# Hybrid decoder trunk on one core: weights streamed in three half chunks, and a ring of eleven slots

## What is computed

```
for layer in range(2):
    hn = rmsnorm(h, attn_norm[layer])
    mix = pool_attention_mixer(...) if layer % 2 == 0 else ssd_mixer(...)
    h = h + mix
    h = h + peer_ffn(rmsnorm(h, ffn_norm[layer]), ...)
```

```
u = expert_u[idx]
act = gelu(einsum('nhkd,nd->nhk', u, xb))
coef = gate * act
out = einsum('nhk,nhkd->nd', coef, expert_v[idx])
```

## Time and profile before

| | |
|---|---|
| median of 3 runs | 1641.92 us (1640.35 to 1643.54) |
| profiled execution | 1642.93 us, span in the profile 1641.1 us |
| TensorE matmul | 1191.8 us busy, 73% |
| VectorE | 1174.9 us, 72% |
| GpSimd | 590.9 us, 36% |
| ScalarE | 522.6 us, 32% |
| DMA | 665.99 MB, mean 406 GB/s |
| of it gathers and other GpSimd DMAs | 540.65 MB, 79.8% of the DMA time |
| of it SP's queue, mostly weights | 123.46 MB, 17.9% |
| granted TensorE clock, mean | 0.869 of full speed |

### The profile page before, as it was taken

One profiled execution on the slowest core, in us unless ns is written; L12 is line 12 of the kernel. 1 busy time (PEld: TensorE's weight loads), 2 busy tenths in 40 slices (PEclk: granted clock), 3 DMA queues, 4 the chain that ended last, 5 costly groups with the idle time before them and its releaser, 6 DMA issues.

```text
span 1641.1 us, 21546 instructions
## 1 busy us (share of the span) xinstructions
PE 1191.8 (73%) x7384; PEld 579.4 (35%) x7384; DVE 1174.9 (72%) x3348; ACT 522.6 (32%) x1207; POOL 590.9 (36%) x525
## 2 busy tenths in 40 slices
PE   8876685768748885978785798599597955555555
PEld 3552232225405662432263366344134611111111
DVE  3557868776678778897665877689966577777755
ACT  0132134222223563642132256355211322222211
POOL 1043333534433223323333432232343444444451
PEclk9987898989968997998998799799798977787776
DMA  9599999999999999999999999999999999999996
GB/s 378 245 375 422 423 423 421 421 422 422 422 412 382 422 423 409 397 422 424 420 423 422 400 422 423 423 403 402 366 412 423 421 421 421 421 421 421 421 421 263
DMA packets 84076, 665.99 MB, mean 406 GB/s; under 512 B 9376, under 2 KB 9520, under 8 KB 10752
## 3 DMA queue, kind: packets, MB, share of 16 engines
q0 software_dynamic: 74608, 540.65, 79.8%
q1 hardware_dynamic: 9216, 123.46, 17.9%
q10 hardware_dynamic: 144, 0.52, 0.1%
HBM read 663.55 MB, written 1.05 MB: 405 GB/s over the span
## 4 chain that ended last, share of the span: by engine, by line
DMA 30%; PE 28%; DVE 26%; ACT 7%; issue 7%; POOL 2%; DVEq 0%; POOLq 0%; ACTq 0%; SPq 0%
DMA ring<-in_experts,idx 30%; PE acc L846 11%; DVE ring L1453 9%; PE act_bank L551 6%; PE dve_bank L537 6%; DVE scratch L1097 3%; ACT L884 2%; DVE onehot L1097 2%; POOL ring L480 2%; ACT scratch L884 2%; ACT diag L1031 1%; DVE scratch L1269 1%; PE act_bank L537 1%; ACT scratch L958 1%; PE act_bank L773 1%
## 5 line engine op out<-in xcount | busy, mean ns | idle before, releaser
L480 POOL DMA_INDIRECT ring<-in_experts,idx x512 | 584.9, 1142 | 1005.3 <-PE acc L846 789.8
L846 PE MATMUL acc<-ring,diag 64*64 64x512 f32 x4096 | 617.8, 731 | 362.3 <-ACT diag L1031 340.6
L1453 DVE CUSTOM_DVE_ANT_0 ring<-ring,hn 128x1024 f32<-128x1024 f32 x512 | 622.4, 1224 | 267.3 <-DMA ring<-in_experts,idx 247.8
L846 PEld LDWEIGHTS acc<-ring,diag 64*64 64x64 f32 x4096 | 155.6, 154 | 723.3 <-ACT diag L1031 468.1
L1024 ACT ACTIVATE acts<-dots 128x2 f32<-128x2 f32 x256 | 52.0, 203 | 720.9 <-DVE dots L1453 703.0
L551 PE MATMUL act_bank<-hnT,wbuf 128*128 128x128 f32 x1856 | 235.3, 285 | 24.9 <-ACT scratch L958 17.4
L551 PEld LDWEIGHTS act_bank<-hnT,wbuf 128*128 128x128 f32 x1856 | 221.8, 198 | 76.3 <-issue 76.3
L1031 ACT ACTIVATE diag<-cst,coefs 128x64 f32<-128x64 f32 x512 | 150.2, 340 | 226.1 <-DVE coefs L1461 191.7
L884 ACT ACT_TABLE_LOAD x80 | 102.6, 1283 | 19.2 <-DMA rowc<-in_rows 16.9
L1461 DVE TENSOR_TENSOR coefs<-acts,gate 128x2 f32<-128x2 f32 x256 | 41.3, 161 | 74.4 <-ACT acts L1024 54.7
L1024 ACT ACT_TABLE_LOAD x68 | 87.2, 1283 | 5.9 <-ACT scratch L884 0.4
(11 more groups left out here) (143 smaller groups left out, 911.2 us busy)
## 6 DMA issues: line engine op xcount, KB each, us to landing
wbuf<-in_weights SPq DMA_DIRECT2D x50, 2048.0 KB
ring<-in_weights SPq DMA_DIRECT2D x5, 2048.0 KB, 19.8
ring<-in_experts,idx POOLq DMA_INDIRECT x512
kept<-in_weights SPq DMA_DIRECT2D x2, 2048.0 KB, 23.6
wbuf<-in_weights SPq DMA_DIRECT2D x2, 1024.0 KB, 7.5
scratch<-in_bias POOLq DMA_DIRECT2D x1, 1024.0 KB, 11.5
scratch<-in_bands POOLq DMA_DIRECT2D x1, 768.0 KB, 13.4
h<-in_x SPq DMA_DIRECT2D x1, 512.0 KB, 4.2
```

The source lines that it names most:

```text
L480: pool.indirect_dma_start(ring[:, n % RING], None, io[f"experts{layer}"], bass.IndirectOffsetOnAxis(idx[:, at:at + 1], 0),).then_inc(sem(f ...
L846: last[rows] = pe.matmul(acc[rows][half][home:home + HALF_P], diag[part, n % DIAGS], ring[part, slot, D + half * CW:D + (half + 1) * CW], ...
L1453: dve.tensor_tensor_reduce(out=ring[:, slot, 0:D], in0=ring[:, slot, 0:D], in1=hn[:, phase % NBLK], scale=1.0, scalar=0.0, op0=ALU.mult, o ...
```

## The change

The two whole buffers become three half buffers of 1 MB (8 KB in each partition). A chunk is loaded by two DMAs, and the halves go round the three buffers. TensorE raises `halves_free` by one for each half that it has read: for the first half on the matmul that reads its last part, for the second where `chunks_free` was raised before. Half m may be loaded once m - 2 releases have come, which is when half m - 3 is read. Chunks read by rows are halved by k. Chunks read by columns (queries and convolution) are stored in memory so that each half holds 256 columns. The 1 MB set free is the eleventh slot of the ring. The first chunk goes to the halves, and chunks 1 to 5 to the ring (chunk 1 was in `wbuf` before, and chunk 6, the first query chunk, in the ring). In the query stage TensorE now also waits for its own product after an even head, before the release.

```diff
-RING = 10
+RING = 11
 GROUP = 2
...
-NWB = 2
+HALVES = 3
 L0_CHUNKS = 4 + 2 + 4
...
-    streamed = 0
+    halves = 0
     for layer in range(DEPTH):
...
                     yield "kept", layer
-                    continue
-                n = streamed
-                streamed += 1
-                if n < NWB:
-                    yield "wbuf", n
-                elif n < NWB + STAGED:
-                    yield "ring", n - NWB
+                elif layer == b == 0 and 1 <= c <= STAGED:
+                    yield "ring", c - 1
                 else:
-                    yield "wbuf", n - STAGED
+                    yield "halves", halves
+                    halves += 2
...
         gains = sb("gains", D)
-        wbuf = sb("wbuf", NWB * CH).rearrange("p (n k c) -> p n k c", n=NWB, k=KD)
+        half_buf = sb("half_buf", HALVES * CH // 2).rearrange("p (n c) -> p n c", n=HALVES)
         ring = sb("ring", RING * 2 * D).rearrange("p (r d) -> p r d", r=RING)
-        staged = ring.rearrange("p (n r) d -> p n (r d)", r=2)
-        kept = sb("kept", CH).rearrange("p (k c) -> p k c", k=KD)
+        staged = ring[:, 0:2 * STAGED].rearrange("p (n r) d -> p n (r d)", r=2)
+        kept = sb("kept", CH)
         cst = sb("cst", C_END)
...
                             sp.wait_ge(sem("bias_loaded"), 16)
-                        if t == 0:
-                            flat = wbuf[:, 0].rearrange("p k c -> p (k c)")
-                            sp.dma_start(flat[:, 0:CH // 2], w[:, 0:CH // 2]).then_inc(sem("half_chunk_in"), 16)
-                            sp.dma_start(flat[:, CH // 2:], w[:, CH // 2:]).then_inc(sem("chunk_in0"), 16)
-                        elif kind == "ring":
+                        if kind == "ring":
                             sp.dma_start(staged[:, n], w).then_inc(sem(f"staged_in{n}"), 16)
...
                                     sp.wait_ge(sem("kept_used"), layer * NBLK)
-                                sp.dma_start(kept.rearrange("p k c -> p (k c)"), w).then_inc(sem("kept_in"), 16)
+                                sp.dma_start(kept, w).then_inc(sem("kept_in"), 16)
                         else:
-                            if n >= NWB:
-                                sp.wait_ge(sem("chunks_free"), n - NWB + 1)
-                            sp.dma_start(wbuf[:, n % NWB].rearrange("p k c -> p (k c)"), w
-                                         ).then_inc(sem(f"chunk_in{n % NWB}"), 16)
+                            for part in range(2):
+                                m = n + part
+                                if m >= HALVES:
+                                    sp.wait_ge(sem("halves_free"), m - HALVES + 1)
+                                sp.dma_start(half_buf[:, m % HALVES], w[:, part * CH // 2:(part + 1) * CH // 2]
+                                             ).then_inc(sem(f"half_in{m % HALVES}"), 16)
                         t += 1
...
         def _(pool):
-            pool.wait_ge(sem("half_chunk_in"), 16)
+            pool.wait_ge(sem("half_in0"), 16)
             pool.dma_start(rowc, io["rows"].to_broadcast([P, 2 * HD + 3 * SH])).then_inc(sem("rows_loaded"), 16)
-            pool.wait_ge(sem("chunk_in1"), 16)
+            pool.wait_ge(sem("staged_in0"), 16)
             pool.dma_start(bias_t, io["bias"].rearrange("p (h k) -> p h k", h=HEADS)).then_inc(sem("bias_loaded"), 16)
...
-                if n % GROUP == 0:
+                if n >= RING and (n - RING) % GROUP == 0 or n == RING:
                     for rows in range(2):
-                        pool.wait_ge(sem(f"pairs_summed{rows}"), n // GROUP + 1)
+                        pool.wait_ge(sem(f"pairs_summed{rows}"), (n - RING) // GROUP + 1 + AHEAD)
                 if n % TOPK == 0:
                     pool.wait_ge(sem("idx_ready"), n // TOPK + 1)
-                if n < RING and n % 2 == 0:
+                if n < 2 * STAGED and n % 2 == 0:
                     pool.wait_ge(sem("staged_free"), n // 2 + 1)
...
-            def next_chunk():
+            class Chunk:
+                def __init__(self, kind, n, by_rows):
+                    self.kind, self.n, self.by_rows, self.seen = kind, n, by_rows, -1
+                    if kind == "kept":
+                        pe.wait_ge(sem("kept_in"), 16 * (n + 1))
+                    if kind == "ring":
+                        pe.wait_ge(sem(f"staged_in{n}"), 16)
+                def half(self, part):
+                    m = self.n + part
+                    if self.kind == "halves":
+                        if part > self.seen:
+                            self.seen = part
+                            pe.wait_ge(sem(f"half_in{m % HALVES}"), 16 * (m // HALVES + 1))
+                        return half_buf[:, m % HALVES]
+                    flat = kept if self.kind == "kept" else staged[:, self.n]
+                    return flat[:, part * CH // 2:(part + 1) * CH // 2]
+                def __getitem__(self, key):
+                    k = key[1]
+                    if self.by_rows:
+                        return self.half(k // (KD // 2)).rearrange("p (k c) -> p k c", k=KD // 2)[:, k % (KD // 2)]
+                    part, first = divmod(key[2].start, CW // 2)
+                    return self.half(part).rearrange("p (k c) -> p k c", k=KD)[:, k, first:first + P]
+                def first_half_read(self, ins):
+                    if self.kind == "halves":
+                        ins.then_inc(sem("halves_free"), 1)
+            def next_chunk(by_rows=True):
                 kind, n = HOMES[chunks[0]]
                 chunks[0] += 1
-                if chunks[0] == 1:
-                    pe.wait_ge(sem("half_chunk_in"), 16)
-                    return wbuf[:, 0]
-                if kind == "kept":
-                    pe.wait_ge(sem("kept_in"), 16 * (n + 1))
-                    return kept
-                if kind == "ring":
-                    pe.wait_ge(sem(f"staged_in{n}"), 16)
-                    return staged[:, n].rearrange("p (k c) -> p k c", k=KD)
-                pe.wait_ge(sem(f"chunk_in{n % NWB}"), 16 * (n // NWB + 1))
-                return wbuf[:, n % NWB]
+                return Chunk(kind, n, by_rows)
...
                 kind = HOMES[chunks[0] - 1][0]
-                pe.sem_inc(sem({"ring": "staged_free", "wbuf": "chunks_free", "kept": "kept_used"}[kind]), 1)
+                pe.sem_inc(sem({"ring": "staged_free", "halves": "halves_free", "kept": "kept_used"}[kind]), 1)
...
                                     stop=last and k == tiles[-1])
+                    if k == KD // 2 - 1 and w is not dtw:
+                        w.first_half_read(ins)
                     if tick is not None and k % 2 and k < tiles[-1]:
...
                                         start=k == 0, stop=k == KD - 1)
+                    if j == 1 and len(tiles) > 2:
+                        w.first_half_read(ins)
                 return ins
...
-                def other_half():
-                    if b == 0:
-                        pe.wait_ge(sem("chunk_in0"), 16)
...
                     ins = yield from row_products(out, hnT, w, tick=T_IN0 + 4 * c,
-                                                  halfway={0: other_half, 3: first_scores}.get(c))
+                                                  halfway=first_scores if c == 3 else None)
                     ins.then_inc(sem(kind + "_full"), 1)
...
                                    bcT[:, (d - 4) * 4:(d - 3) * 4].rearrange("p g t -> p (g t)"), 4)
-                    w = next_chunk()
+                    w = next_chunk(by_rows=False)
                     out = fill("act")
...
                                 ins = pe.matmul(out_z, hnT[:, k], w[:, k], start=k == 0, stop=k == KD - 1)
+                                if k == KD // 2 - 1:
+                                    w.first_half_read(ins)
                     if g < SG and g % 2:
...
                     if hd % 2 == 0:
-                        w = next_chunk()
+                        w = next_chunk(by_rows=False)
                     out = fill("act")
...
                     ins.then_inc(sem("act_full"), 1)
-                    if hd % 2:
+                    if hd % 2 or w.kind == "halves":
                         chunk_used("act")
...
+def by_column_halves(chunks):
+    n = len(chunks)
+    return chunks.reshape(n, P, KD, 2, CW // 2).transpose(0, 1, 3, 2, 4).reshape(n, P, CH)
...
         consts[:, C_GAIN + layer * KD:C_GAIN + (layer + 1) * KD] = tiles_last(a["attn_norm"][layer])
-    weights = [chunked(np.concatenate([q_and_k, pooled, v], axis=1)), chunked(a["even_w_out"][0]), chunked(a["peer_w_q"][0]),
-               chunked(w_in[:, SI:SI + XBC]), chunked(w_in[:, 0:SI]), chunked(a["ssm_w_out"][0]),
-               chunked(a["peer_w_q"][1])]
+    weights = [chunked(np.concatenate([q_and_k, pooled, v], axis=1)), chunked(a["even_w_out"][0]), by_column_halves(chunked(a["peer_w_q"][0])),
```

(2 more changed lines are left out.)

## The result

The changed kernel takes 1645.8 us (median of 20 executions, 1643.3 to 1648.1), the kernel before on the same chips 1643.3 us (20 executions): ratio 1.0018, 95% interval 1.0011 to 1.0024. It is some 3 us slower, where I had forecast 7.1 us faster. The profiled execution took 1648.1 us, with a span of 1646.3 us.

What follows compares the result with a forecast made beforehand. The prediction took the DMA engines, at 422 GB/s, to bound the kernel. Slot -9.6, weights' room +2.5 and other terms 0 summed to -7.1 us, so a median of 1634.8 us, range 1626 to 1644.

Steps and rivals of the forecast that it cites:

- the first dip: DMA rate below 422 GB/s from 480 to 510 us: 5.0 us lost, forecast to shrink to about 2.5 us.
- The slot: Eleventh ring slot: one more gather allowed ahead, worth at most 2.48 us once per stretch, together 9.6 us saved.
- A: Stretch from 474.6 to 548.9 us where no dot product waits for a gather: 5.0 us lost, 2.48 us to win.
- B: Stretch from 626.4 to 763.4 us where no dot product waits for a gather: 3.9 us lost, 2.48 us to win.
- D: Stretch from 1053.0 to 1193.7 us where no dot product waits for a gather: 10.6 us lost, 2.48 us to win.
- C: Stretch from 899.0 to 971.9 us where no dot product waits for a gather: 2.1 us lost, all to win.
- The room of the weights: Three half chunks of room for four: one half load moves from the idle start into full DMA time, plus 2.48 us.
- the old gap: DMA idle time at the start, from 64 us to the first gather at 84.19 us; weights were forecast to move there.
- Halving and the number of transfers: Weight loads: a half chunk costs 2.48 us at 422 GB/s like a gather, and 50 more DMAs cost nothing.
- rival 3: Halves come late in the 16 convolution chunks, TensorE waits 0.5 us for each of 32: +16 us, 1651 us; chance 0.13.
- Rival 1: In the stretches, half a chunk less ahead takes back 0 to 5 us of the slot's 9.6: 1639.4 to 1644.4; chance 0.20.
- Rival 2: In the dips, more comes back: half of the remaining 12 us gives 1628.8, all of it 1622.8 us; chance 0.15.

Runs made afterwards that it cites:

- the second run: The changed kernel run once more, unchanged, beside the kernel before, with a second profile taken: ratio 1.0023 (1.0014 to 1.0033).
- after: The changed kernel (three half buffers, eleven slots) against the kernel before: 1645.8 us, ratio 1.0018.
- the pair with the lighter convolution: Changed kernel with two of three convolution taps on VectorE left out, against the kernel before: 1.0026 with ten slots, 0.9999 with eleven.
- four halves: Changed kernel with four half buffers and ten slots, the memory of the kernel before, only halved: 1647.5 us, ratio to before 1.0029.
- two halves: Changed kernel with two half buffers and twelve slots: ratio to the kernel before 1.0107 (1.0091 to 1.0122).

## Why the prediction was wrong, point by point

**What bounds the kernel.** That the DMA is the level at which it runs, and that only idle DMA time can be won, held. What failed is the yardstick: "each as length times (1 - rate / 422)". This is the mean over 16 engines, and a gather waits for the last of them. By the last parts, of the 5.0 us that I gave to the first dip, 2.3 were time of the last engine; of the 2.1 of the third, 0.7. The rest was time of the engines ahead, and filling it brought nothing here. The deeper ring made it plain: the first dip filled up to 404 GB/s, gathers took 19.4 us from issue to landing for 16.8 with ten slots, and the time hardly moved.

**The slot, -9.6 forecast, -4.1 measured** (-3.3 by the second run). The failed step is "A, B and D: 2.48 us each; C: 2.1 us". A and C gave nothing. B and D gave about 5 us by the landings, of which D alone 3.5 (3.9 with the second profile of after, 4.2 in the pair with the lighter convolution): more than one gather, against my "once, however many dips the stretch has". The stretches are not of fixed length either. With ten slots and three halves D ran from 1057.1 to 1198.1 us, with eleven from 1056.2 to 1205.5. A stretch ends where the engines have used up what had landed ahead, so another slot makes it longer. Halving moves it too: B took 137.0 us before, 142.6 with ten slots and three halves.

**The room of the weights, +2.5 forecast, +2.3 measured.** Right within a wide interval, and the mechanism is in the traces. The 101 GB/s in the old gap, which I had named as its sign, don't show it: four halves move them too, and they have the old room. What shows it is the bytes: when the first gather lands, SP's queue has moved 21.7 MB before and with four halves, and 20.7 MB with three, one half chunk less. SP issued the missing half at 92.2 us (forecast 91.5). From there on, with 2.49 us for each half chunk set off, three halves run 1.6 us behind four at the first gather, 2.2 at gather 145 and 1.8 at the last (the least between them is -0.2, at gather 280).

**Halving and the number of transfers, 0 forecast, +4.8 measured.** The failed step is that a half "costs the same 2.48 us" beside the gathers: I took 422 GB/s for any mixture of pieces, though the row for it (100 to 480 us) is mostly gathers. In the stretches of the weights before had 423, and every kernel with 8 KB pieces whose loads were in time 420 or 421. Over the two stretches shown that is 1.6 us, and 6.1 us of packet time over the whole run; that it is the whole of the 4.8 us is argued, not shown. Nor is the number of transfers settled: a second DMA for each chunk adds 1.8 us by the ratios, which the intervals can't tell from nothing. The fixed cost that the Trainium skill ("DMA: Bandwidth & Descriptors", Anatomy of one DMA) gives, about 2.0 us for each DMA on GpSimd's path, would make an estimated 100 us of 50 more if it were exposed. These loads are on SyncE's, and two DMAs for each chunk cost 3.3 us in all. With this term and the slot as measured the sum is +3.0; with the slot as forecast it would have been -2.3.

**Halves in time, 0 forecast.** Right. No wait for `half_buf` appears on TensorE, and rival 3 is refuted for three halves; two halves show it. Where a half loads, the weights had 56.9% of the DMA time in 533 to 536 us and 52.4% in 539 to 542, near the half that I had expected. Queues, changed kernel, 539 to 542 us:

```profile
q1 hardware_dynamic: 80, 0.66, 52.4%
q0 software_dynamic: 81, 0.61, 49.2%
```

The Trainium skill's rule ("DMA: Bandwidth & Descriptors", Queues, rings and completion order) that an engine goes round its queues packet by packet agrees with it. In the kernel before I read 72.2% against 28.4% as such turns, near two to one. It is 2.5 to one, 94 packets of 16 KB against at most 71 of 8 KB, so in those 5 us the turns were not one for one.

**TensorE's additions, 0 forecast.** Not isolated. TensorE's idle time ahead of the key products, which follow the new wait, went from 35.4 to 41.1 us (before, then after):

```profile
L827 PE MATMUL act_bank<-keysT,scratch 128*128 128x128 f32 x128 | 23.0, 304 | 35.4 <-issue 25.5
L844 PE MATMUL act_bank<-keysT,scratch 128*128 128x128 f32 x128 | 24.4, 318 | 41.1 <-ACT scratch L901 28.2
```

That is inside my bound of 8.1 us. Whether any of it reached the time no run tells; it would be part of the 4.8 us. The 0.1 us that I gave each new wait stands in no row.

**The rivals.** Rival 1 gave 1639.4 to 1644.4 by a trade of room against slot. The trade is there (2.3 against 4.1 us), but it isn't what made the kernel slower. Rival 2 is refuted: B and D kept their dips.

## What to carry to other kernels

A transfer spread over 16 DMA engines is done when the last part is in: read a dip in the mean GB/s only after the landings of first and last parts, since it may be engines ahead that wait for the one behind, and then more depth fills the dip and not the time. Before cutting a stream into smaller pieces, read the rate in a stretch where it is mixed with the other traffic, not the rate of that traffic alone. And when room is moved from one buffer to another, take apart the cutting, the room lost and the room won in runs of their own: here they were +4.8, +2.3 and -4.1 us, none of which the total of +3 would have told.

## What the runs showed of the hardware

- Pieces of 16 KB beside gathers of 8 KB: 423 GB/s. Pieces of 8 KB: 420 to 421. Pieces of 4 KB: 392 to 394, though there loads were late too (DMA share 0.98 for 1.01).
- The parts of a gather land mostly 2 to 9 us apart (at most 12.2), and while the queues never run empty the gap doesn't close: in the last phase it went from 3.7 to 8.5 us in the changed kernel. 48 packets of 0.61 us, by all signs on one engine, opened it to 12.7 us, and the run took 28.3 us longer.
- Queue q8 brings TensorE's instructions, one packet of 16 KB for 280 increments. Some q8 packets coincide with a slip of some 1 us in the part of one engine. Queue q14 brings instructions of SyncE, 21 packets of 8 KB for some 5200 waits, which cost nothing that could be measured (1.0002). The steps of 1 us in the gap of the last phase come with packets of q14 beside which a gather packet takes 0.97 us for 0.31; no run isolates their price.
- Sixteen rows of 16 KB loaded at once took 0.77 to 2.1 us each (mean 1.44), a single one 0.61 us.
